# Second layer of a two-layer trunk: its first four mixing and up-projection units taken on the unnormalised input, root and shift applied to their sums, its modulation vectors all on VectorE

## The chip, the cores and the metric

The kernel runs on one core of one Trainium2 chip. The metric is device time in microseconds (us) of one execution. Engines are called as in the profile: PE is TensorE (PEld its weight loads), DVE is VectorE, ACT is ScalarE, POOL is GpSimd, SP is the engine whose queue issues nearly all DMAs.

## What is computed

Two layers run over 384 tokens (128 context, 256 latent), D = 1024. Cut to what matters here, a layer is:

```
mod = silu(cond) @ w_ada + b_ada              # six vectors: sh1, sc1, g1, sh2, sc2, g2
h   = rms(x, g_norm1) * (1 + sc1) + sh1
u   = h @ w_in                                # gates and the inputs of four token mixers
...                                           # mixers, branch projections, gated merge
x   = x + g1 * (merged @ w_out)
h2  = rms(x, g_norm2) * (1 + sc2) + sh2
x   = x + g2 * (silu(gate) * val) @ w_down    # gate, val: conv of width 3 over h2 @ w_up
```

rms divides a token by the root of its mean square. `cond` is one vector for context tokens and another for latent tokens, so each modulation vector has two columns. All is float32.

## The kernel before

**Layout.** Activations are transposed: 8 blocks (k = 0 to 7) of 128 channels by 384 tokens. Weights come as a stream of units, one unit being one block of 128 output channels: 128 x 1024 in SBUF, 512 KB. Layer l has 13 mixing units, 32 gate units, 8 branch, 8 output (`O0`), 44 up-projection (`P0`) and 24 down-projection units (`D0`, three to a block d of x). Every product is made of three: weight and activation are split in a high and a low part, and `dense` (L1439) gives PE three products per block k: high by high, high by low, low by high, so 24 products of 384 columns for a whole unit.

**Weight pipeline.** A unit passes four slots. SP loads it (`load_unit`, L478) once the unit four before is done, ACT rounds it to the high part (`split`, L687), DVE subtracts for the low part (`split`, L976), and PE waits for both in `unit_ready` (L1434). All four queues run in the order in which the program is written; nothing reorders them.

**Norms.** For layer 2's first norm and for the second norm of both layers, x gets its last block from the last `residual` (DVE, L1317). Then: ACT squares it, PE sums squares over channels with a matrix of ones (`square_sums`, L1471), ACT takes the root with Ln and Exp (L714 to L716), and then per block DVE multiplies x by scale and root (L1047), ACT adds the shift and rounds (`act_hi`, L725), DVE makes `act_lo` (L1055). PE starts the next stage with `group` (L1452), three units interleaved over k, each step waiting for its block's `act_lo`.

**Modulation.** The vectors come in two ways. Some are PE products against `cond_silu` (`modulate`, L1396, 8 blocks of 512 KB each): in layer 2 these are sh2 (`hole_units`, between the first norm's square sums and its first unit) and g2 (`norm_units`, at the same place of the second norm). The others are row products on DVE (`row_products`, L1000), two instructions for a 512 KB block, spread between the splits by `MIX_ROWS`, `STEP_ROWS` and `DOWN_LAST`; SP loads block b once the two products of block b - 2 are done (L443).

**MLP.** An up unit's bank is read by ACT (the middle tap, L914) and DVE (the outer taps, L1350 and L1354), in pairs of units; DVE finishes a column block with L1359 and L1362, then splits the next unit but one (L1363). PE may write bank j again only after the convolution of its last unit, and units `P0+4` to `P0+7` use banks 0 to 3 again (L1829).

## Time and profile before

| what | value |
|---|---|
| median of 3 runs (lowest to highest) | 1223.99 us (1223.44 to 1224.53) |
| the profiled execution | 1223.51 us |
| its span | 1221.7 us |
| PE busy | 1208.0 us, 99% of the span |
| DVE busy | 901.4 us, 74% |
| ACT busy | 575.6 us, 47% |
| POOL busy | 136.8 us, 11% |
| HBM read | 195.25 MB, 162 GB/s over the span |

The span is the part of the execution from the first to the last recorded instruction; the execution's own time is 1.8 us more. The page gives busy times of each engine; a chain of waits, followed back from the last instruction, tells what set the end; a timeline lists instructions with their start in us from the start of the span, and in brackets how long the engine sat idle before and what ended that. Layer 1 ends and layer 2 begins at about 620 us; layer 2's second norm lies at about 938 us.

### The profile page before, as it was taken

What the parts mean: (1) busy time and instruction counts of PE and PEld (TensorE: products, weight loads), DVE (VectorE), ACT (ScalarE), POOL (GpSimd) and SP (SyncE); (2) the same over time, 40 slices, a digit from 0 to 9 for tenths busy, and PEclk for the clock granted to TensorE, in tenths of its full rate; (3) what the DMA queues carried; (4) which work ended last, traced back from release to release, by engine and by line L of the source; (5) the groups of instructions that cost most, each with busy time, mean ns of one, the idle gap of its engine ahead of it and who ended that gap; (6) DMA issues with size and microseconds to landing.
All of it is one profiled execution on the core that took longest, in us unless ns stands there. A gap on an engine that the chain in (4) does not pass through costs nothing.

```text
span 1221.7 us, 19781 instructions
## 1 busy us (share of the span) xinstructions
PE 1208.0 (99%) x7816; PEld 1149.7 (94%) x7816; DVE 901.4 (74%) x1671; ACT 575.6 (47%) x949; POOL 136.8 (11%) x109
## 2 busy tenths in 40 slices
PE   8999999999999999999999999999999999999998
PEld 7987999989989999999989889999998999999998
DVE  5597877748689999986876965765686887887432
ACT  3445564643365544532354455645425554454321
POOL 0232000008300000000202500000271000000000
PEclk9999999999999999999999999999999999999999
DMA  9763433444744444469664522332345334334443
GB/s 370 291 220 125 147 117 112 172 139 161 253 173 144 167 156 159 169 216 322 214 234 163 189 87 87 104 104 87 104 167 196 122 124 135 122 123 136 134 142 121
DMA packets 53532, 198.82 MB, mean 163 GB/s; under 512 B 6784, under 2 KB 7200, under 8 KB 51904
## 3 DMA queue, kind: packets, MB, share of 16 engines
q1 hardware_dynamic: 53120, 196.86, 46.0%
q8 instruction: 63, 1.03, 0.3%
q0 software_dynamic: 320, 0.69, 0.2%
q14 instruction: 29, 0.24, 0.1%
HBM read 195.25 MB, written 2.27 MB: 162 GB/s over the span
## 4 chain that ended last, share of the span: by engine, by line
PE 93%; DVE 2%; POOL 2%; DMA 1%; issue 1%; ACT 0%; SPq 0%; DVEq 0%; POOLq 0%; ACTq 0%
PE bank L1444 27%; PE bank L1446 27%; PE bank L1445 26%; PE bank L1743 1%; PE bank L1723 1%; PE bank L1512 1%; DVE w_lo L980 1%; DMA start_ada<-start_ada 1%; PE bank L1517 1%; PE bank L1516 1%; POOL wide L653 1%; PE bank L1713 1%; POOL merge_sum L655 1%; PE bank L1501 1%; PE bank L1698 1%
## 5 line engine op out<-in xcount | busy, mean ns | idle before, releaser
L1444 PE MATMUL bank<-act_hi,w_hi 128*128 128x384 f32 x1368 | 465.0, 340 | 0.7 <-DVE act_lo L1055 0.3
L1446 PE MATMUL bank<-act_hi,w_lo 128*128 128x384 f32 x1368 | 457.8, 335 | 0.0
L1445 PE MATMUL bank<-act_lo,w_hi 128*128 128x384 f32 x1336 | 446.6, 334 | 0.0
L980 DVE TENSOR_TENSOR w_lo<-w_raw,w_hi 128x1024 fp32r<-128x1024 f32 x251 | 318.9, 1272 | 114.6 <-ACT w_hi L662 113.6
L662 ACT ACTIVATE w_hi<-w_raw 128x1024 fp32r<-128x1024 f32 x251 | 264.3, 1054 | 167.8 <-DMA w_raw<-stream 167.7
L1444 PEld LDWEIGHTS bank<-act_hi,w_hi 128*128 128x128 f32 x1368 | 257.1, 188 | 10.7 <-issue 6.5
L1446 PEld LDWEIGHTS bank<-act_hi,w_lo 128*128 128x128 f32 x1368 | 256.8, 188 | 0.0
L1445 PEld LDWEIGHTS bank<-act_lo,w_hi 128*128 128x128 f32 x1336 | 251.0, 188 | 0.6
L1446 PE MATMUL bank<-mlp_hi,w_lo 128*128 128x384 f32 x352 | 118.3, 336 | 0.0
L1444 PE MATMUL bank<-mlp_hi,w_hi 128*128 128x384 f32 x352 | 118.3, 336 | 0.0
L1445 PE MATMUL bank<-mlp_lo,w_hi 128*128 128x384 f32 x352 | 118.3, 336 | 0.0
L1350 DVE SCALAR_TENSOR_TENSOR mlp_tmp<-bank,params,mlp_tmp 128x127 f32<-128x127 f32 (+1 forms) x176 | 64.7, 409 | 38.1 <-ACT mlp_tmp L662 38.1
L662 ACT ACTIVATE mlp_tmp<-bank,params 128x384 f32<-128x384 f32 x88 | 54.2, 667 | 81.3 <-PE bank L1446 81.3
L1354 DVE SCALAR_TENSOR_TENSOR mlp_tmp<-bank,params,mlp_tmp 128x127 f32<-128x127 f32 (+1 forms) x176 | 65.2, 412 | 3.1
L1444 PEld LDWEIGHTS bank<-mlp_hi,w_hi 128*128 128x128 f32 x352 | 66.2, 188 | 0.0
L1446 PEld LDWEIGHTS bank<-mlp_hi,w_lo 128*128 128x128 f32 x352 | 66.2, 188 | 0.0
L1445 PEld LDWEIGHTS bank<-mlp_lo,w_hi 128*128 128x128 f32 x352 | 66.2, 188 | 0.0
L1011 DVE SCALAR_TENSOR_TENSOR row_products<-ada,cond_spread 128x1024 f32<-128x1024 f32 x48 | 60.9, 1270 | 0.9 <-DMA ada<-ada_rows 0.7
L1238 DVE TENSOR_REDUCE small<-bank 128x1 f32<-128x384 f32 (+1 forms) x72 | 31.3, 462 | 40.9 <-PE bank L1714 15.6
L662 ACT ACTIVATE gates_b<-bank 128x384 f32<-128x384 f32 x48 | 23.6, 492 | 67.6 <-PE bank L1446 67.3
L1011 DVE SCALAR_TENSOR_TENSOR row_products_mix<-ada,cond_spread_mix 128x1024 f32<-128x1024 f32 x38 | 50.9, 1340 | 4.0 <-DMA cond_spread_mix<-cond_rows 3.1
L653 POOL TENSOR_TENSOR wide<-wide 128x768 f32<-128x768 f32 x8 | 18.7, 2334 | 273.7 <-DVE wide L1306 273.7
(246 smaller groups left out, 1576.0 us busy)
## 6 DMA issues: line engine op xcount, KB each, us to landing
w_raw<-stream SPq DMA_DIRECT2D x251, 512.0 KB, 3.3
ada<-ada_rows SPq DMA_DIRECT2D x48, 512.0 KB, 4.4
start_ada<-start_ada SPq DMA_DIRECT2D x8, 1024.0 KB, 17.9
ada_norm<-ada_w SPq DMA_DIRECT2D x16, 512.0 KB, 5.8
ada<-ada_w SPq DMA_DIRECT2D x8, 512.0 KB, 5.5
start_raw<-start_w SPq DMA_DIRECT2D x8, 448.0 KB, 18.5
ada_head_a<-ada_w SPq DMA_DIRECT2D x5, 512.0 KB, 7.3
cond_spread_mix<-cond_rows SPq DMA_DIRECT2D x2, 1024.0 KB, 7.9
```

The costliest lines, as they stand in the source:

```text
L653: own(nc.gpsimd.tensor_tensor(g[:, 0:2, :], g[:, 0:2, :], g[:, 2:4, :], ALU.add))
L655: nc.gpsimd.tensor_tensor(msum[:, d % 4, :], g[:, 0, :], g[:, 1, :], ALU.add).then_inc(merged_ready, 1)
L662: return nc.scalar.activation(out, in_, func, **kw)
L980: V.tensor_tensor(wlo[s][:, :], raw[s][:, :], whi[s][:, :].bitcast(F32), ALU.subtract).then_inc(lo_ready, 1)
L1011: V.scalar_tensor_tensor(out[:, :], ada[b % 2][:, :], 1.0, tile[:, t, :], ALU.mult, ALU.mult, accum_out=mod[:, at, t:t + 1]).then_inc(rows ...
L1238: own(V.reduce_max(small[:, c + m:c + m + 1], bank[score_bank(i, m)][:, 0:n], AX))
L1350: own(V.scalar_tensor_tensor(f[:, m, a + 1:e], b[:, a:e - 1], before, f[:, m, a + 1:e], ALU.mult, ALU.add))
L1354: ins = V.scalar_tensor_tensor(f[:, m, a:e - 1], b[:, a + 1:e], behind, f[:, m, a:e - 1], ALU.mult, ALU.add)
L1444: T.matmul(out, wb[s][0][:, w, :], hi[k], start=first and k == 0, stop=False)
L1445: T.matmul(out, wb[s][0][:, w, :], lo[k], start=False, stop=False)
L1446: ins = T.matmul(out, wb[s][1][:, w, :], hi[k], start=False, stop=last and k == n - 1)
L1501: ins = T.matmul(bank[7][p0:p0 + STRIP, j * n:(j + 1) * n], conds[:, k, :], w[:, c:c + n], start=k == 0, stop=k == KD - 1)
```

## The change

Layer 1 computes as before. In layer 2, for both norms:

- **Four units on the unnormalised input** (`FIRST = 4`). As each block of x gets final, ACT writes x times scale to `gated_late`, rounds it to a new tile `unnormed_hi`, and DVE makes `unnormed_lo` (`unnormed_high`, `unnormed_low`). Two more columns behind the 384 hold the shift vector. PE runs the four first units one after another on these tiles, 386 columns wide, with the square sums after block 3 of the first unit (`first_units`).
- **Root and shift on the sums.** For each of the four, DVE copies the two shift columns and multiplies the 384 sums by the root (`rescale`), ACT adds the shift columns (`add_shift`), in place in the bank for the up units.
- **The normalised input** for all later units is still made: POOL multiplies `gated_late` by the root into `wide` (`normed`, 8 instructions), ACT rounds (`normed_high`), DVE makes `act_lo` (`normed_low`). These are written between the rescales and splits. The fifth unit waits for them block by block (`normed_unit`).
- **Modulation.** `hole_units` and layer 2's `norm_units` are gone from PE. sh2 and g2 of layer 2 are 16 more blocks of row products: eight more in the mixing and attention stages, eight in the up projection; the 26 row products of layer 1's down projection are the first ones again but start two units later and are spread by `DOWN_ROWS`, from a copy of the condition loaded over `act_hi`.
- Output projection block d % 4 = 3 uses bank 6 in place of bank 0.

In the diff, `act.` and `A(` stand in ACT's program, `dve.` and `V.` in DVE's, `pe.` and `dense` in PE's.

```diff
-DOWN_LAST = (2, 2, 1, 1, 1, 1, 1, 1)
+DOWN_ROWS = [0, 0] + [1 + (u in (5, 10, 15, 20)) for u in range(2, 24)]
-            {u: 1 for u in range(5, 21)})
-STEP_ROWS = ({0: 1, 1: 1, 2: 1, 3: 1, 13: 2, 14: 2, 15: 2, 16: 2, 17: 2}, {})
+            {u: 1 + (u == 10) for u in range(6, 23)})
+STEP_ROWS = ({0: 1, 1: 1, 2: 1, 3: 1, 13: 2, 14: 2, 15: 2, 16: 2, 17: 2},) * 2
-OUT_BANK = (2, 5, 4, 0)
+OUT_BANK = (2, 5, 4, 6)
...
+                def normed(n):
+                    pool.wait_ge(rstd_ready, l * 2 + n + 1)
+                    for k in range(KD):
+                        nc.gpsimd.tensor_tensor(wide[:, k, :], late[:, k, :], rsn, ALU.mult).then_inc(norm_full, 1)
...
+                def unnormed_high(n, d):
+                    for a, e, c in RANGES:
+                        ins = A(late[:, d, a:e], x[:, d, a:e], ACT.Copy, scale=(sc1, sc2)[n][:, d, c:c + 1])
+                    ins.then_inc(u_full, 1)
+                    act.wait_ge(u_full, n * KD + d + 1)
+                    A(uhi[n][:, d, 0:TOK], late[:, d, :], ACT.Copy).then_inc(u_hi, 1)
+                def add_shift(n, q, out):
+                    act.wait_ge(rescaled, n * FIRST + q + 1)
+                    for a, e, c in RANGES:
+                        ins = A(out[:, a:e], out[:, a:e], ACT.Identity, bias=sums_shift[:, q, c:c + 1])
+                    return ins
...
                         for m in range(2):
+                                add_shift(1, 2 * j + m, bank[2 * j + m]).then_inc(shifted, 1)
+                                act.wait_ge(shifted, 2 * j + m + 1)
                             A(f[:, m, :], bank[2 * j + m][:, 0:TOK], ACT.Identity,
+                        if l > 0 and i == 0 and j == 0:
+                            normed_high(1, 3)
+                            normed_high(1, 4)
                         A(f[:, 2, :], f[:, 0, :], ACT.Tanh, scale=0.5).then_inc(mlp_tanh, 1)
                         split(u + 4, i)
+                            for k in range(5, KD):
+                                normed_high(1, k)
...
+                    if l < DEPTH - 1 and u % 3 == 0 and u >= 6:
+                        d = u // 3 - 2
+                        act.wait_ge(x2_ready, FROM + l * KD + d + 1)
+                        unnormed_high(0, d)
...
+                def rescale(n, q, out):
+                    u = (0, P0)[n] + q
+                    dve.wait_ge(rstd_ready, l * 2 + n + 1)
+                    dve.wait_ge(unit_done, FROM + l * UNITS + u + 1)
+                    V.tensor_copy(sums_shift[:, q, :], bank[q][:, TOK:wide_w])
+                    V.tensor_tensor(out, bank[q][:, 0:TOK], rsn, ALU.mult).then_inc(rescaled, 1)
...
                         split(u + 3, i)
+                        if l > 0 and i == 0 and j == 0:
+                            normed_low(1, 2)
+                            rescale(1, 1, bank[1][:, 0:TOK])
+                            normed_low(1, 3)
+                            normed_low(1, 4)
+                        if l > 0 and i == 0 and j == 1:
+                            rescale(1, 2, bank[2][:, 0:TOK])
+                            rescale(1, 3, bank[3][:, 0:TOK])
...
-            def hole_units():
...
+                def first_units(n, u0, ready, counts):
+                    for q in range(FIRST):
+                        unit_ready(u0 + q)
+                        pe.wait_ge(ready, counts[q])
+                        for k in range(KD):
+                            if q == 0:
+                                pe.wait_ge(u_lo, n * (KD + 1) + k + 1 + (n == 1 or k >= 3))
+                            ins = dense(bank[q][:, 0:wide_w], u0 + q, [k], [uhi[n][:, k, :]], [ulo[n][:, k, :]], k == 0, k == KD - 1)
+                            if q == 0 and k == 3:
+                                square_sums(n)
+                        ins.then_inc(unit_done, 1)
...
-                    square_sums(0)
-                    hole_units()
-                    group(0, (0, 1, 2), HI, LO, lambda k: pe.wait_ge(norm_lo, l * 2 * KD + k + 1))
+                    first_units(0, 0, x2_ready, [FROM + KD // 2 + 1 + q for q in range(FIRST)])
```

**First place: DVE at the end of layer 1's down projection.** Before, with the last two blocks of x (`x<-bank` is a residual, `row_products` a row product, the two `w_lo` are the splits of units 0 and 1 of layer 2):

```order
L1011 SCALAR_TENSOR_TENSOR row_products,mod<-ada_65,cond_spread 128x1024 [waits rows_read,rows_loaded0]
L1319 SCALAR_TENSOR_TENSOR x<-bank,mod,x 128x128 [waits unit_done]
L1319 SCALAR_TENSOR_TENSOR x<-bank,mod,x 128x256
L1011 SCALAR_TENSOR_TENSOR row_products,mod<-ada_65,cond_spread 128x1024 [waits rows_read]
L1011 SCALAR_TENSOR_TENSOR row_products,mod<-ada_66,cond_spread 128x1024 [waits rows_read,rows_loaded1]
L1011 SCALAR_TENSOR_TENSOR row_products,mod<-ada_66,cond_spread 128x1024 [waits rows_read]
L980 TENSOR_TENSOR w_lo_59<-w_raw_60,w_hi_61 128x1024 [waits hi_ready]
L980 TENSOR_TENSOR w_lo_62<-w_raw_63,w_hi_64 128x1024 [waits hi_ready]
L1319 SCALAR_TENSOR_TENSOR x<-bank,mod,x 128x128 [waits unit_done]
L1319 SCALAR_TENSOR_TENSOR x<-bank,mod,x 128x256
```

And now:

```order
L1097 SCALAR_TENSOR_TENSOR row_products_down,mod<-ada_66,cond_spread_down 128x1024 [waits rows_read,spread_down_loaded]
L1097 SCALAR_TENSOR_TENSOR row_products_down,mod<-ada_65,cond_spread_down 128x1024 [waits rows_read,rows_loaded0]
L1432 SCALAR_TENSOR_TENSOR x<-bank,mod,x 128x128 [waits unit_done]
L1432 SCALAR_TENSOR_TENSOR x<-bank,mod,x 128x256
L1069 TENSOR_TENSOR unnormed_lo_112<-gated_late,unnormed_hi_111 128x384 [waits unnormed_hi]
L1097 SCALAR_TENSOR_TENSOR row_products_down,mod<-ada_65,cond_spread_down 128x1024 [waits rows_read,spread_down_loaded]
L1097 SCALAR_TENSOR_TENSOR row_products_down,mod<-ada_66,cond_spread_down 128x1024 [waits rows_read,rows_loaded1,spread_down_loaded]
L1097 SCALAR_TENSOR_TENSOR row_products_down,mod<-ada_66,cond_spread_down 128x1024 [waits rows_read,spread_down_loaded]
L1066 TENSOR_TENSOR w_lo_59<-w_raw_60,w_hi_61 128x1024 [waits hi_ready]
L1066 TENSOR_TENSOR w_lo_62<-w_raw_63,w_hi_64 128x1024 [waits hi_ready]
L1432 SCALAR_TENSOR_TENSOR x<-bank,mod,x 128x128 [waits unit_done]
L1432 SCALAR_TENSOR_TENSOR x<-bank,mod,x 128x256
```

Two row products instead of one stand ahead of the residual of block 6, an `unnormed_lo` piece follows it, and then come the three row products, the two splits and the last residual as before.

**Second place: SP at the same point.** Before, from the load of unit `D0+23` to that of unit 3 of layer 2 (`ada<-ada_rows` is a block for the row products):

```order
L483 DMA w_raw_54<-stream 128x1024 [waits unit_done]
L446 DMA ada_65<-ada_rows 128x1024 [waits rows_read]
L483 DMA w_raw_57<-stream 128x1024 [waits unit_done]
L483 DMA w_raw_60<-stream 128x1024 [waits unit_done]
L446 DMA ada_66<-ada_rows 128x1024 [waits rows_read]
L483 DMA w_raw_63<-stream 128x1024 [waits unit_done]
L483 DMA w_raw_54<-stream 128x1024 [waits unit_done]
L483 DMA w_raw_57<-stream 128x1024 [waits unit_done]
```

And now:

```order
L490 DMA w_raw_57<-stream 128x1024 [waits unit_done]
L490 DMA w_raw_60<-stream 128x1024 [waits unit_done]
L453 DMA ada_65<-ada_rows 128x1024 [waits rows_read]
L490 DMA w_raw_63<-stream 128x1024 [waits unit_done]
L453 DMA ada_66<-ada_rows 128x1024 [waits rows_read]
L490 DMA w_raw_54<-stream 128x1024 [waits unit_done]
L490 DMA w_raw_57<-stream 128x1024 [waits unit_done]
```

The last block of rows is issued behind the load of layer 2's unit 1, no longer ahead of it.

**Third place: DVE in layer 2's MLP**, from the split of unit `P0+3` to that of unit `P0+4`. Before:

```order
L980 TENSOR_TENSOR w_lo_59<-w_raw_60,w_hi_61 128x1024 [waits hi_ready]
L1350 SCALAR_TENSOR_TENSOR mlp_tmp<-bank,params,mlp_tmp 128x127 [waits tap1]
L1350 SCALAR_TENSOR_TENSOR mlp_tmp<-bank,params,mlp_tmp 128x255
L1354 SCALAR_TENSOR_TENSOR mlp_tmp<-bank,params,mlp_tmp 128x127 [waits dve_own]
L1354 SCALAR_TENSOR_TENSOR mlp_tmp<-bank,params,mlp_tmp 128x255
L1350 SCALAR_TENSOR_TENSOR mlp_tmp<-bank,params,mlp_tmp 128x127 [waits tap1]
L1350 SCALAR_TENSOR_TENSOR mlp_tmp<-bank,params,mlp_tmp 128x255
L1354 SCALAR_TENSOR_TENSOR mlp_tmp<-bank,params,mlp_tmp 128x127 [waits dve_own]
L1354 SCALAR_TENSOR_TENSOR mlp_tmp<-bank,params,mlp_tmp 128x255
L1359 SCALAR_TENSOR_TENSOR mlp_tmp<-mlp_tmp 128x384 [waits mlp_tanh]
L1362 SCALAR_TENSOR_TENSOR mlp_tmp<-mlp_tmp 128x384 [waits conv_val,dve_own]
L980 TENSOR_TENSOR w_lo_62<-w_raw_63,w_hi_64 128x1024 [waits hi_ready]
```

And now, up to the first outer tap (the rest, taps to `P0+4`'s split, is as before and is followed by three more pieces of `act_lo`):

```order
L1066 TENSOR_TENSOR w_lo_59<-w_raw_60,w_hi_61 128x1024 [waits hi_ready]
L1133 SCALAR_TENSOR_TENSOR act_lo<-wide,mod,act_hi 128x128 [waits norm_hi]
L1133 SCALAR_TENSOR_TENSOR act_lo<-wide,mod,act_hi 128x256
L1153 COPY cond_raw<-bank 128x2 [waits unit_done,rstd_ready]
L1154 TENSOR_TENSOR bank<-bank,rstd 128x384
L1133 SCALAR_TENSOR_TENSOR act_lo<-wide,mod,act_hi 128x128 [waits norm_hi]
L1133 SCALAR_TENSOR_TENSOR act_lo<-wide,mod,act_hi 128x256
L1133 SCALAR_TENSOR_TENSOR act_lo<-wide,mod,act_hi 128x128 [waits norm_hi]
L1133 SCALAR_TENSOR_TENSOR act_lo<-wide,mod,act_hi 128x256
L1483 SCALAR_TENSOR_TENSOR mlp_tmp<-bank,params,mlp_tmp 128x127 [waits tap1]
```

Between the split and the taps stand three pairs of `act_lo` and a rescale. The second column block has two rescales between the split of `P0+5` and its taps.

## Rows read from the trace of the kernel before

**Rows 1.** The page: busy time of each engine.

```profile
PE 1208.0 (99%) x7816; PEld 1149.7 (94%) x7816; DVE 901.4 (74%) x1671; ACT 575.6 (47%) x949; POOL 136.8 (11%) x109
```

**Rows 2.** The chain of waits, 615 to 640 us: start, length, what.

```profile
620.16 0.75 DVE x L1319 x2
...
621.37 1.05 ACT w_hi L662
622.44 1.23 DVE w_lo L980
623.73 0.76 DVE wide L1047 x2
624.57 0.81 ACT act_hi L662 x2
625.48 0.76 DVE act_lo L1055 x2
626.27 0.44 PE bank L1444
```

**Rows 3.** Timeline of PE where layer 2 begins: start, busy, engine, line, operation.

```profile
619.96 0.81 PE L1474 MATMUL bank<-wide,consts 128*128 128x384 f32 x2
620.61 0.81 PE L1476 MATMUL bank<-wide,consts 128*128 128x384 f32 x2
```

**Rows 4.** Timeline of DVE, then PE, where layer 2's MLP begins.

```profile
933.57 0.74 DVE L1319 SCALAR_TENSOR_TENSOR x<-bank,mod,x 128x128 f32<-128x128 f32 x2 [2.29 <-PE bank L1446]
...
937.73 0.74 DVE L1319 SCALAR_TENSOR_TENSOR x<-bank,mod,x 128x128 f32<-128x128 f32 x2 [2.28 <-PE bank L1446]
...
937.53 0.81 PE L1474 MATMUL bank<-wide,consts 128*128 128x384 f32 x2
...
943.69 0.44 PE L1444 MATMUL bank<-act_hi,w_hi 128*128 128x384 f32 x1
```

**Rows 5.** Timeline of DVE at the end of layer 1's down projection.

```profile
609.99 1.93 DVE L980 TENSOR_TENSOR w_lo<-w_raw,w_hi 128x1024 fp32r<-128x1024 f32 x1 [1.11 <-ACT w_hi L662]
611.84 1.21 DVE L1011 SCALAR_TENSOR_TENSOR row_products<-ada,cond_spread 128x1024 f32<-128x1024 f32 x1
...
612.98 0.73 DVE L1319 SCALAR_TENSOR_TENSOR x<-bank,mod,x 128x128 f32<-128x128 f32 x2
...
617.38 2.35 DVE L980 TENSOR_TENSOR w_lo<-w_raw,w_hi 128x1024 fp32r<-128x1024 f32 x2
```

**Rows 6.** Timeline of SP at the same place; the page's row on the ada rows.

```profile
609.09 0.43 SPq L446 DMA_DIRECT2D ada<-ada_rows  x1
612.88 7.61 SPq L483 DMA_DIRECT2D w_raw<-stream  x3
...
ada<-ada_rows SPq DMA_DIRECT2D x48, 512.0 KB, 4.4
```

**Rows 7.** Timeline of ACT: a table load; the middle taps of two up units.

```profile
609.97 1.28 ACT L666 ACT_TABLE_LOAD   x1
...
960.67 1.21 ACT L662 ACTIVATE mlp_tmp<-bank,params 128x384 f32<-128x384 f32 x2
```

**Rows 8.** Timeline of DVE in the first two column blocks of layer 2's MLP.

```profile
959.17 1.22 DVE L980 TENSOR_TENSOR w_lo<-w_raw,w_hi 128x1024 fp32r<-128x1024 f32 x1
960.31 0.55 DVE L983 TENSOR_TENSOR mlp_lo<-mlp_tmp,mlp_hi 128x384 fp32r<-128x384 f32 x1
...
961.94 0.73 DVE L1350 SCALAR_TENSOR_TENSOR mlp_tmp<-bank,params,mlp_tmp 128x127 f32<-128x127 f32 x2
...
965.85 1.22 DVE L980 TENSOR_TENSOR w_lo<-w_raw,w_hi 128x1024 fp32r<-128x1024 f32 x1
```

**Rows 9.** Timeline of POOL, then DVE: instructions alone and beside each other.

```profile
609.82 1.01 POOL L589 TENSOR_TENSOR wide<-wide 128x384 f32<-128x384 f32 x1
...
907.06 2.18 DVE L1289 SCALAR_TENSOR_TENSOR merged_lo<-merge_sum,merged_hi 128x384 fp32r<-128x384 f32 x1
910.70 0.56 DVE L1289 SCALAR_TENSOR_TENSOR merged_lo<-merge_sum,merged_hi 128x384 fp32r<-128x384 f32 x1 [1.47 <-ACT merged_hi L662]
```

More of the change, by code:

```diff
@@ L361, in program @@
         norm_ada_loaded = [sem(f"norm_ada_loaded{n}") for n in range(2)]
-        hole_ada_loaded = [sem(f"hole_ada_loaded{n}") for n in range(2)]
+        spread_down_loaded, scale_ready = sem("spread_down_loaded"), sem("scale_ready")
+        u_full, u_hi, u_lo, rescaled = sem("unnormed_full"), sem("unnormed_hi"), sem("unnormed_lo"), sem("rescaled")
+        shifted = sem("shifted")
         rows_loaded = [sem(f"rows_loaded{n}") for n in range(2)]
@@ L719, in norm @@
+                def norm(n):
+                    roots(n)
                     for k in range(KD):
-                        if n == 0 and l == 0:
+                        if n == 0:
                             start_high(k)
                             act.wait_ge(start_shift, k + 1)
-                        act.wait_ge(norm_full, (l * 2 + n) * KD + k + 1)
-                        for a, e, c in RANGES:
-                            ins = A(ahi[:, k, a:e], wide[:, k, a:e], ACT.Identity, bias=shift[:, k, c:c + 1])
@@ L756, in _ @@
                     if name in SQUARED:
-                        i, rows = SQUARED.index(name), NOPE if name == "cqr" else P
-                        act.wait_ge(mix_out, l * U_MIX + u + 1)
-                        A(wide[0:rows, i, :], pj[0:rows, PJ[name], :], ACT.Square).then_inc(psq, 1)
+                        mix_squares(u)
                 def gate(g):
@@ L1102, in _ @@
                 else:
-                    dve.wait_ge(shift_ready, l)
-                    norm(0)
-                    modulation(l, 3)
+                    for u in range(FIRST):
+                        rescale(0, u, pj[:, PJ[MIX[u]], :])
+                        normed_low(0, 2 * u)
+                        if u < FIRST - 1:
+                            split(u + 3)
+                        normed_low(0, 2 * u + 1)
                 def lambdas():
@@ L1363, in _ @@
                         split(u + 4, i)
+                        if l > 0 and i == 0 and j == 0:
+                            for k in range(5, KD):
+                                normed_low(1, k)
                         dve.wait_ge(mlp_hi, p + 1)
@@ L1519, in start_products, with normed_unit @@
                             ins.then_inc(unit_done, 1)
+                def first_units(n, u0, ready, counts):
[9 more added lines that the diff above has]
+                        ins.then_inc(unit_done, 1)
+                def normed_unit(out, u, n):
+                    unit_ready(u)
+                    for k in range(KD):
+                        pe.wait_ge(norm_lo, (l * 2 + n) * KD + k + 1)
+                        ins = dense(out, u, [k], HI[k:k + 1], LO[k:k + 1], k == 0, k == KD - 1)
+                    ins.then_inc(unit_done, 1)
                 if l == 0:
```

286 lines of the change are left out of this document (185 added, 101 removed).

## The prediction

> **What bounds the kernel now.** I read the page first: PE is busy 99% of the span, DVE 74%, ACT 47% [rows 1]. So only what PE executes, and the few stretches in which it waits, can move the end. The second view is the chain of waits where layer 2 begins. It leaves PE and runs, one after another, through the last residual, ACT's high part of a weight unit, DVE's low part, and then the norm's own steps: `wide`, `act_hi`, `act_lo`, first product [rows 2]. The third view, PE's timeline, gives the length: the square sums start at 619.96 and follow each other every 0.65 us, so three take 1.95; the first dense product starts at 626.27 [rows 2, 3]. That is a hole of 6.31 us, in which the removed `hole_units` only fill time. At the second norm of layer 2 it is 937.53 to 943.69, 6.16 us [rows 4]. DVE's residuals there lie 4.16 us apart, which is a full unit of 24 products, 0.173 us each [rows 4]. Everything below is measured against this beat.
>
> **What a perfect change would bring.** The sums stay on PE (1.95 us). Without any wait the holes shrink to that: 6.31 - 1.95 = 4.4 us and 6.16 - 1.95 = 4.2 us. The modulation products of layer 2 stood inside the holes, so their removal is in these numbers and is no gain of its own. The question is what is late next. Both places must be walked through queue by queue.
>
> **First place, start of layer 2.** PE wants unit 0 at 619.96. Before, DVE split units 0 and 1 together from 617.38 to about 619.7, the first done near 618.55 [rows 5]. Now its queue is longer: one more row product ahead of the residual of block 6, 1.25 us (before, three of them fill the time from the residual's end, 613.64, to 617.38 [rows 5]); one `unnormed_lo` piece, 0.5 us (nearest row: a low part of the same size, 0.55 busy [rows 8]). Besides, the last block of rows is issued behind the unit load of 612.88 and no longer at 609.09; at 4.4 us to landing it is there at 617.7 [rows 6], while DVE wants it at 612.98 + 1.25 + 0.7 + 0.5 + 1.25 = 616.7. That is 1.0 us more. Sum: 618.55 + 1.25 + 0.5 + 1.0 = 621.3. ACT isn't later: after the residual (615.0) it has the scaled block and its rounding, 0.81 + 0.55, the table load, 1.28, and the high part, 1.05, thus 618.7 [rows 2, 7]. So PE waits 1.35 us (bounds: 0.3 if the block lands in time, 2.3 if it needs a microsecond more), and the hole shrinks by 6.31 - 1.95 - 1.35 = 3.0 us. The last block of x costs nothing: PE needs it only as step 7 of unit 0, some 6 us after its start, and ACT and DVE need 3 to 4 us from the last residual.
>
> The four units then end at 621.3 + 1.95 + 4 x 4.16 = 639.9. Unit 4 needs the third rescaled sum out of the way. From the root (628) DVE has three rescales (0.7 each, taken as a low part of 384 elements and a small copy; bounds 0.5 and 1.1, two such), four `act_lo` pairs of 0.76 and two splits of 1.2: 7.5 us, 635.5 [rows 2, 8]. But POOL now runs its eight products in the same time. **What POOL costs DVE** the trace shows: beside a POOL add, a split took 1.93 in place of 1.22, and a 384-element low part 2.18 in place of 0.56 [rows 5, 8, 9]. I take 0.7 us for each of the six pieces: 639.7, and with ACT's shift, 0.81 [rows 2], 640.5. PE waits 0.6 us (bounds 0 and 2). The two added columns cost 192 x 2/384 x 0.173 = 0.2 us over both places, 0.1 here. First place: -3.0 + 0.6 + 0.1 = **-2.3 us** (-4.4 to -0.5).
>
> **Second place, start of layer 2's MLP.** PE starts unit `P0` at 937.53 with no wait: the DMA queue lost eight modulation blocks there, and DVE's splits have 2.3 us of idle time around each residual [rows 4]. The four units end at 937.53 + 1.95 + 16.64 = 956.1, before at 943.69 + 16.64 = 960.3. Then `P0+4` needs its low part. Before, that split ran 959.17 to 960.31 [rows 8]: ready in the very moment. It stands in DVE's queue behind the convolution of units 0 and 1, and now four more things stand ahead of that. Step by step: sums done 941.6, root 942.7, table load to 944.0 [rows 7], three `act_hi` and the high part of `P0+3` to 947.5; DVE's split to 948.7, `act_lo` and rescale of unit 1 to 950.2; then back to ACT: shift 0.81, tap 0.6, two `act_hi` 1.6, to 953.2 [rows 2, 7]; back to DVE: `act_lo` to 954.0, taps and the rest of the column block 3.9 us (961.94 to 965.85 [rows 8]), to 957.9, split to 959.1. With POOL beside it for two of these pieces and more, 1.4 us, **960.5**. So the part that gates PE is as late as before: of the 4.2 us nothing is left (bounds: 959.1 without POOL, 962 with it throughout).
>
> And the queue is longer in the next half block too. Before, from the split of `P0+4` to the end of that of `P0+6` were 960.31 to 967.0, 6.7 us [rows 8], against two units, 8.3 us. Now: three `act_lo` 2.2, low part 0.5, split 1.15, one rescale, the shift and the tap behind it 2.1 (the other rescale beside them), taps and rest 3.9, split 1.15: 11.0 us. PE waits 2.7 us, `P0+6` starts at 960.5 + 11.0 = 971.5, before at 960.3 + 8.3 = 968.65. Second place: **+2.8 us** (+1.3 to +4.3). Afterwards a half block takes DVE 6.7 us, with a row product 7.9, against 8.3: it catches up, and the eight blocks of row products that come into this stage cost nothing. Those in mixing and attention go to places where layer 1's tables already have as many; if that cover is gone, each costs its 1.25 us.
>
> **The sum.** 1223.5 (the profiled execution) - 2.3 + 2.8 = 1224.0. That execution lies 0.5 below the median of the runs, so **1224.5 us**. A measurement of this kernel can tell about 0.2%, 2.4 us, from no change; this is inside it. By its own bounds this case reaches from 1221.5 to 1228.
>
> **Rivals.** (1) *The queues keep up*, faster. If the pieces of ACT and DVE overlap better than I chain them and the low part of `P0+4` is ready at 956 to 957, `P0+6` is in time too; the second place gives up to -4.2 and the first -3: 1216.8. For it: DVE has 26% idle in all [rows 1]. Against: DVE and ACT wait for each other in turn through shift, tap, `act_hi`, `act_lo`, and the split was just in time even before [rows 8].
> (2) *POOL locks DVE out*, slower. The eight POOL products stand back to back, about 1.0 us each [rows 9], from 942.7 on. If every DVE instruction with two SBUF inputs waits for the end of one of them, as the 2.18 us row suggests [rows 9], the split of `P0+3` and the three pairs ahead of the second rescale are later by some 3 us and not 1.4, and unit 4 of layer 2 waits 2 us longer: second place +4.5, first -0.3, 1228.2. It decides once `P0+4`'s low part comes after 962. The Trainium skill, "SBUF — State Buffer", section "SBUF: two separate sides", says that VectorE with two SBUF inputs and GpSimd take a shared port pair for the whole instruction and the other one fully blocks; by that rule the time is this rival's. The forecast takes the smaller price because of the eight pieces only some meet an add at its start, and sums in PSUM take one SBUF input.
> (3) *The 386-column form is slow.* If it ran at the square sums' beat, 0.325 a product in place of 0.173 [rows 3, 4], 192 of them would cost 29 us: 1253. Same operands and type speak against it.
>
> **How the numbers follow.** The forecast's case has 0.52: 0.38 within 0.2%, 0.10 slower, 0.04 faster, since its bounds lean upward. Rival 1 has 0.24, rival 2 0.21, rival 3 0.03. So faster 0.28, same 0.38, slower 0.34. The range, 1218.5 to 1229.0, takes in the forecast's bounds and rival 2, and leaves out the far half of rival 1 and rival 3.
>
> **What would show it.** In the new profile PE should start layer 2's unit 0 about 1.3 us after the last down product, waiting for `w_lo`, and unit `P0` with no wait. It should wait for DVE `w_lo` about 4.4 us ahead of `P0+4` (956.1 to 960.5, shifted by the 2.3 us won) and 2.7 us ahead of `P0+6`; those two waits are the forecast. Products of 386 columns should come every 0.174 us. DVE splits beside POOL's eight products should take about 1.9 us. I am wrong if either MLP wait is missing, if PE waits inside a first unit for `unnormed_lo`, or if a wait appears in attention, where rows were added.

## The result, and the profile after

The changed kernel takes **1233.32 us** (median of 4 runs, 1231.78 to 1234.43), the kernel before, on the same chip, 1223.81 (1223.44 to 1224.53): a ratio of 1.0075, 95% interval 1.0062 to 1.0087. It is 9.5 us slower. The prediction said 1224.5, which is almost no change, and a range up to 1229.0. The forecast is wrong and the range misses the time by 4.3 us.

The page of the changed kernel answers [rows 1]: PE lost a point, DVE is 46 us busier, and the granted clock of PE, full in every slice before, is not full in one of the 40 slices.

```profile
PE 1206.8 (98%) x7688; PEld 1150.2 (93%) x7688; DVE 947.1 (77%) x1735; ACT 597.4 (48%) x1011; POOL 154.0 (12%) x125
...
PEclk9999999999999999999999999999999899999999
```

The view by windows says where. Columns: window, length, busy time and instructions of PE, PEld, DVE, ACT and POOL, then PE's granted clock, DMA share and GB/s.

```profile
620.00:630.00 10.00, 8.09 (x33) 6.66 (x32) 6.30 (x10) 5.52 (x10) 0.58 (x1) 0.83 0.86 326
630.00:640.00 10.00, 10.00 (x58) 10.00 (x57) 9.32 (x12) 7.12 (x17) 9.45 (x12) 1.00 0.54 184
640.00:650.00 10.00, 7.36 (x39) 6.28 (x37) 9.95 (x16) 5.11 (x13) 7.43 (x7) 1.00 0.29 100
...
960.00:970.00 10.00, 4.31 (x15) 4.02 (x14) 9.89 (x24) 5.17 (x11) 0.00 (x0) 0.74 0.16 53
```

Three stretches lose, and DVE is full in two of them. PE's timeline shows both kinds of loss, waits and pace. The products of one unit follow each other every 0.18 us until 623.41, and from there every 0.32, although nothing is waited for:

```profile
622.28 0.41 PE L1581 MATMUL bank<-unnormed_hi,w_hi 128*128 128x386 f32 x1 [1.91 <-ACT w_hi L673]
...
623.06 0.34 PE L1582 MATMUL bank<-unnormed_lo,w_hi 128*128 128x386 f32 x1
...
623.41 0.52 PE L1581 MATMUL bank<-unnormed_hi,w_hi 128*128 128x386 f32 x1
623.73 0.52 PE L1582 MATMUL bank<-unnormed_lo,w_hi 128*128 128x386 f32 x1
...
648.16 0.44 PE L1581 MATMUL bank<-act_hi,w_hi 128*128 128x384 f32 x1 [2.24 <-DVE act_lo L1133]
649.35 0.44 PE L1581 MATMUL bank<-act_hi,w_hi 128*128 128x384 f32 x1 [0.40 <-DVE act_lo L1133]
...
966.35 0.66 PE L1581 MATMUL bank<-act_hi,w_hi 128*128 128x384 f32 x1 [5.69 <-DVE w_lo L1066]
...
1037.30 0.41 PE L1581 MATMUL bank<-act_hi,w_hi 128*128 128x384 f32 x1 [1.72 <-ACT w_hi L673]
```

The slow pace is the lower of TensorE's two levels, 1.2 GHz in place of 2.4; this text calls it half pace. Behind the first wait it lasts about 3.4 us, from 623.4 to 626.8, and costs 1.7: from the start of unit 0 to its 14th product, square sums included, PE takes 5.9 us (622.28 to 628.18), and 4.24 for the same work at the second place (941.54 to 945.78). Behind 966.35 it lasts 5.2 us and costs 2.5.

The profile puts the wait of 1.91 us down to ACT's `w_hi`. Unit 0 had its high part at 620.38; its low part, the first of the two splits here, stands behind the last row product and was ready near 622.1:

```profile
619.80 1.23 DVE L1097 SCALAR_TENSOR_TENSOR row_products_down<-ada,cond_spread_down 128x1024 f32<-128x1024 f32 x1
620.95 2.36 DVE L1066 TENSOR_TENSOR w_lo<-w_raw,w_hi 128x1024 fp32r<-128x1024 f32 x2
```

Unit 4 starts without a wait, at 643.02, and stops 15 products later, at block 5 of the normalised input. Its `act_lo` is the last line here, and the three pieces run beside POOL's window sums of mixing:

```profile
642.05 2.17 DVE L1133 SCALAR_TENSOR_TENSOR act_lo<-wide,mod,act_hi 128x128 fp32r<-128x128 f32 x2
644.14 1.88 DVE L1066 TENSOR_TENSOR w_lo<-w_raw,w_hi 128x1024 fp32r<-128x1024 f32 x1
645.94 2.16 DVE L1133 SCALAR_TENSOR_TENSOR act_lo<-wide,mod,act_hi 128x128 fp32r<-128x128 f32 x2
```

How late each mark is against the kernel before gives the account (starts of instructions, in us; the last column adds up what came in since the mark above):

| mark | before | after | late | what came in between |
|---|---|---|---|---|
| last down product of layer 1 starts | 619.79 | 620.03 | 0.2 | before the places; not explained |
| mixing, product behind the root | 674.90 | 678.41 | 3.5 | wait 1.9, half pace 1.7, unit 4's waits 2.6, wait for the root 0.45, wide columns 0.4, some 0.6 in short pauses around the waits; less the 4.4 of the hole |
| `P0`, before the square sums ahead of it, starts | 937.53 | 941.54 | 4.0 | short waits that before doesn't have, the longest 0.3 at 924.8 |
| unit `P0+4` starts | 960.49 | 966.35 | 5.9 | wait 5.7, columns 0.4; less the 4.2 |
| unit `P0+6` starts | 968.89 | 977.16 | 8.3 | half pace 2.5 |
| end of the span | 1221.7 | 1232.6 | 10.9 | wait 1.7 at 1037 |

(Of the last line 0.9 us is not accounted for.) DVE's timeline at the second place shows what takes its time while POOL runs its eight products, 947.0 to 956.4:

```profile
949.09 2.22 DVE L1133 SCALAR_TENSOR_TENSOR act_lo<-wide,mod,act_hi 128x128 fp32r<-128x128 f32 x2 [2.59 <-ACT act_hi L673]
951.24 0.14 DVE L1153 COPY cond_raw<-bank 128x2 f32<-128x2 f32 x1
951.30 0.55 DVE L1154 TENSOR_TENSOR bank<-bank,rstd 128x384 f32<-128x384 f32 x1
951.77 1.75 DVE L1133 SCALAR_TENSOR_TENSOR act_lo<-wide,mod,act_hi 128x128 fp32r<-128x128 f32 x2
953.44 2.05 DVE L1066 TENSOR_TENSOR w_lo<-w_raw,w_hi 128x1024 fp32r<-128x1024 f32 x1
955.40 1.50 DVE L1133 SCALAR_TENSOR_TENSOR act_lo<-wide,mod,act_hi 128x128 fp32r<-128x128 f32 x2
...
947.02 9.34 POOL L597 TENSOR_TENSOR wide<-gated_late,rstd 128x384 f32<-128x384 f32 x8 [6.64 <-ACT rstd L673]
```

A pair of `act_lo` is 0.75 [rows 2], a split 1.22 [rows 8]. The four pieces are late by 1.5 + 1.0 + 0.8 + 0.75 = 4.0 us. The rescale, which reads one of its inputs from PSUM, keeps its 0.55. The Trainium skill, "SBUF — State Buffer", section "SBUF: two separate sides", says that of a VectorE instruction with two SBUF inputs and a GpSimd instruction that reads SBUF the one that starts first holds their shared ports to its end, and the other is blocked. The trace agrees: a POOL product takes 1.17 us here, and a pair of `act_lo`, two instructions, takes up to 2.22 us in place of 0.75.

### The profile page after: what moved, and what is told of

It reads as the page before. It is cut to its first block, busy times and chain, and to the rows that moved or that the text cites. A ratio compares the mean times of both kernels' runs of the same rounds, so it can differ in the third digit from the quotient of the medians.

```text
span 1232.6 us, 19718 instructions
## 1 busy us (share of the span) xinstructions
PE 1206.8 (98%) x7688; PEld 1150.2 (93%) x7688; DVE 947.1 (77%) x1735; ACT 597.4 (48%) x1011; POOL 154.0 (12%) x125
## 3 DMA queue, kind: packets, MB, share of 16 engines
q8 instruction: 62, 1.02, 0.3%
HBM read 197.35 MB, written 2.27 MB: 162 GB/s over the span
## 4 chain that ended last, share of the span: by engine, by line
PE 87%; DVE 6%; DMA 4%; ACT 2%; issue 1%; SPq 0%; POOL 0%; DVEq 0%; ACTq 0%
PE bank L1581 25%; PE bank L1583 24%; PE bank L1582 24%; DMA w_raw<-stream 2%; DVE w_lo L1066 2%; DVE act_lo L1133 1%; PE bank L1902 1%; PE bank L1882 1%; PE bank L1649 1%; DMA start_ada<-start_ada 1%; PE bank L1654 1%; PE bank L1653 1%; PE bank L1872 1%; ACT w_hi L673 1%; PE bank L1638 1%
## 5 line engine op out<-in xcount | busy, mean ns | idle before, releaser
L1581 PE MATMUL bank<-act_hi,w_hi 128*128 128x384 f32 x1304 | 445.3, 341 | 10.3 <-DVE w_lo L1066 5.7
L1583 PE MATMUL bank<-act_hi,w_lo 128*128 128x384 f32 x1304 | 437.4, 335 | 0.0
L1582 PE MATMUL bank<-act_lo,w_hi 128*128 128x384 f32 x1272 | 426.3, 335 | 0.0
L1581 PEld LDWEIGHTS bank<-act_hi,w_hi 128*128 128x128 f32 x1304 | 245.9, 189 | 21.2 <-issue 14.0
L1583 PEld LDWEIGHTS bank<-act_hi,w_lo 128*128 128x128 f32 x1304 | 245.5, 188 | 0.0
L1582 PEld LDWEIGHTS bank<-act_lo,w_hi 128*128 128x128 f32 x1272 | 239.8, 189 | 0.6
L1097 DVE SCALAR_TENSOR_TENSOR row_products_mix<-ada,cond_spread_mix 128x1024 f32<-128x1024 f32 x44 | 55.1, 1253 | 4.4 <-DMA cond_spread_mix<-cond_rows 3.7
L673 ACT ACTIVATE mlp_tmp<-mlp_tmp 128x384 f32<-128x384 f32 x44 | 23.1, 525 | 61.0 <-DVE mlp_tmp L1487 61.0
```

The lines of the kernel that those rows point to most:

```text
L673: return nc.scalar.activation(out, in_, func, **kw)
L1097: V.scalar_tensor_tensor(out[:, :], ada[b % 2][:, :], 1.0, tile[:, t, :], ALU.mult, ALU.mult, accum_out=mod[:, at, t:t + 1]).then_inc(rows ...
L1581: T.matmul(out, wb[s][0][:, w, :], hi[k], start=first and k == 0, stop=False)
L1582: T.matmul(out, wb[s][0][:, w, :], lo[k], start=False, stop=False)
L1583: ins = T.matmul(out, wb[s][1][:, w, :], hi[k], start=False, stop=last and k == n - 1)
```

## The experiments

All diffs are against the changed kernel and abridged. Each ratio is against the kernel before, run on the same chip; its medians there are 1223.8 to 1224.3 us. Differences between two variants are taken from their medians; where the two intervals overlap, as for several below, the time alone does not separate them. The traces show single executions.

**e1: only the modulation moved.** Both norms as before, the row products where the change has them.

```diff
-                    first_units(0, 0, x2_ready, ...)
+                    square_sums(0)
+                    group(0, (0, 1, 2), HI, LO, lambda k: pe.wait_ge(norm_lo, l * 2 * KD + k + 1))
```

> Both norms of layer 2 as in the kernel before (no unit on the unnormalised input), but the modulation stays on VectorE as in the change, so that each hole holds nothing but three square sums: PE is idle for about 4.3 us in it. Theory 'clock' (PE loses its granted clock behind an idle stretch and runs at half pace for some 4 to 5 us, which costs 2.2 to 2.6 us): 1223.8 + 2 x 2.4 = 1228.6, and with the late weight unit behind the rows of the MLP, 1.7, 1230.3; slices behind both holes show a granted clock under 1. Rival 'the modulation is free and the clock is set by something else': 1223.8 to 1225.5, granted clock 1.00 throughout.

Measured 1232.02 (ratio 1.0063, 1.0048 to 1.0078), above even the first theory. **Taking the modulation off PE, with the new places of its row products, costs 8 us by itself.** Windows of PE alone:

```profile
620.00:630.00 10.00, 3.53 (x11) 0.80 0.94 351
630.00:640.00 10.00, 10.00 (x52) 0.86 0.12 48
...
950.00:960.00 10.00, 10.00 (x50) 0.83 0.11 46
```

The rest comes from DVE and PE around the first hole:

```profile
622.44 0.73 DVE L1471 SCALAR_TENSOR_TENSOR x<-bank,mod,x 128x128 f32<-128x128 f32 x2
...
623.78 0.91 PE L1672 MATMUL bank<-wide,consts 128*128 128x384 f32 x2 [2.69 <-ACT wide L683]
628.48 0.69 PE L1638 MATMUL bank<-act_hi,w_hi 128*128 128x384 f32 x1 [3.78 <-DVE act_lo L1156]
```

The last residual comes at 622.44, before at 620.16 [rows 2]: one more row product and two waits for its block (0.64 and 0.70) stand ahead of it. Behind the holes PE runs at the low level, which costs 2.1 us at the first and 1.7 at the second, and in mixing it waits 1.1 us for a root.

**e5: the same, with the holes filled.** The products of constants return to PE what the modulation did for it: something to run.

```diff
+                    for _ in range(16):
+                        T.matmul(bank[7][:, 0:P], cc("ones"), cc("ones"), start=True, stop=True)
```

> The kernel of e1 (both norms as before, modulation on VectorE) with 16 small products of constants behind the square sums of each norm of layer 2 (3.5 us of the 3.8 that PE waits there). Theory 'clock': nothing is earlier or later on VectorE and ScalarE, only the half pace behind the holes goes: granted clock 1.00, 1232.0 - 4.2 = 1227.8; what is left against before (3.5 to 4) are the last residual of layer 1, 2.3 us late behind a row product, and the 1.1 us for the root in mixing. Rival 'the time of e1 is the row products alone': 1231 to 1232.

Measured 1228.63 (1.0041, 1.0026 to 1.0056): 3.4 us less than e1, from products that compute nothing (the intervals of the two overlap a little). The second hole is followed by full clock; the first still has a slice at 0.83, since the fill stands behind a wait of 2.8 us inside the sums.

```profile
620.00:630.00 10.00, 7.21 (x37) 0.83 0.85 318
630.00:640.00 10.00, 10.00 (x62) 1.00 0.22 90
...
950.00:960.00 10.00, 10.00 (x60) 1.00 0.09 22
```

**e2: fill in the changed kernel** (8 products ahead of unit 0, 25 behind the bank's wait of `P0+4`).

> The change, with 8 small products of constants ahead of layer 2's unit 0 (1.7 us) and 25 ahead of unit P0+4 (5.4 us), into a bank nobody reads: they lie inside the waits that the changed kernel has there (1.9 and 5.7 us). Theory 'clock': the waits stay, the half pace behind them goes, granted clock 1.00, 1233.3 - 4.8 = 1228.5. Rival 'the clock falls for another reason' (the 386-column products, the DMA load): same clock record, 1233 to 1234.

Measured 1231.25 (1.0057, 1.0042 to 1.0072); in the profiled execution the clock is 1.00 throughout. 2.1 us came back and not 4.8, and the interval overlaps that of the changed kernel. The filler of the second place started only at 961.28, when the bank was free, and ran 2 us past the low part; e8 mends that.

**e8: the fill where PE really stands** (24 products ahead of that wait).

> e2 with the filler of the second place (24 products, 5.2 us) ahead of the wait for bank 0, where PE really stands, so that it ends before the low part comes. Theory 'clock': 2.2 us (first place) and 2.6 us (second place) come back in full, 1228.5; in e2 the filler ran 961.3 to 966.9, 2.1 us beyond the low part. Rival 'the second place has no clock loss of its own': 1231.

Measured 1233.51 (1.0074, 1.0059 to 1.0089): nothing. Its trace is the most telling of all:

```profile
966.44 0.41 PE L1638 MATMUL bank<-act_hi,w_hi 128*128 128x384 f32 x1 [0.30 <-DVE w_lo L1089]
977.15 0.41 PE L1638 MATMUL bank<-act_hi,w_hi 128*128 128x384 f32 x1 [2.12 <-DVE w_lo L1089]
```

Full clock behind 966.44, and `P0+6` then waits 2.1 us for its low part and starts at 977.15, where the changed kernel has 977.16. The half pace there had only hidden the wait of the forecast. At the first place the low level now came behind unit 4's wait instead (slices of 0.96 and 0.87 from 640).

**e9: GpSimd's presence alone.**

```diff
-                        nc.gpsimd.tensor_tensor(wide[:, k, :], late[:, k, :], rsn, ALU.mult).then_inc(norm_full, 1)
+                        nc.gpsimd.tensor_tensor(wide[:, k, 0:2], late[:, k, 0:2], rsn[:, 0:2], ALU.mult).then_inc(norm_full, 1)
```

> The change, with GpSimd multiplying only 2 of the 384 columns of each block of a norm of layer 2 by the root (the other columns reach the high and low parts with whatever wide holds): its eight operations take next to nothing, and nobody else does their work. It leaves out the normalisation of those columns. It prices GpSimd's presence alone. Theory 'port': VectorE's pairs and splits beside GpSimd return to 0.75 and 1.22 us, some 4 us at each norm; unit 4's wait goes, P0+4's falls from 5.7 to about 2; P0+6 waits 0 to 1: 1233.3 - 2.6 - 2.2 - 3.7 = 1225 to 1227. Rival 'chain of shift, tap and split': P0+4 waits 4 us or more all the same, 1230.

The other 382 columns are not normalised here: e9 is a price and not a version.

Measured 1225.47 (1.0017, 1.0007 to 1.0026), 10 runs: **of the 9.5 us, 7.9 are gone once eight operations a norm shrink, on an engine that is idle 88% of the time.** Not all of that is POOL's. The two traces lie 8.8 us apart. Of these, 0.5 stands already at the last down product; 1.7 is the half pace of the first place, which did not follow here although PE waited 2.12 us ahead of unit 0, all before POOL's first product at 627.56; and 1.7 is the wait at 1037, which e1 and e3 lack too. About 4.9 us are left, 3.7 of them between the start of `P0` and that of `P0+6`. That is what POOL's products do to VectorE and, since ScalarE's `act_hi` waits for each, their own length. The clock is 1.00 throughout in this trace. The same pieces as above, and what is left of the waits:

```profile
946.33 0.75 DVE L1179 SCALAR_TENSOR_TENSOR act_lo<-wide,mod,act_hi 128x128 fp32r<-128x128 f32 x2 [2.59 <-ACT act_hi L686]
...
948.66 1.23 DVE L1112 TENSOR_TENSOR w_lo<-w_raw,w_hi 128x1024 fp32r<-128x1024 f32 x1 [0.40 <-ACT w_hi L686]
```

```profile
960.00 0.41 PE L1696 MATMUL bank<-act_hi,w_hi 128*128 128x384 f32 x1 [2.09 <-DVE w_lo L1112]
970.71 0.41 PE L1696 MATMUL bank<-act_hi,w_hi 128*128 128x384 f32 x1 [2.14 <-DVE w_lo L1112]
```

2.1 + 2.1 us: just what the hole had given. Even with GpSimd's products away the second place gains nothing.

**e3: the eight products on VectorE.**

> The change, with the eight products x times root of each norm of layer 2 on VectorE in place of GpSimd. Theory 'port' (VectorE with two SBUF inputs waits for GpSimd's operation): pairs of act_lo 0.75 us in place of 1.2 to 2.4, unit 4's wait of 2.6 us goes, the wait ahead of P0+4 falls from 5.7 to 2 to 4 us; 1233.3 - 2.6 - 2.5 = 1228. Rival 'length of the queue': VectorE has 16 more operations of 0.5 us, 4 us a norm, which eat what the pairs give back: both waits as long as now or longer, 1233 to 1236.

Measured 1229.7 (1.0041, 1.0026 to 1.0056). The pairs are 0.75 us again, except beside POOL's window sums of mixing, the products take 3.9 us a norm, and the whole is 3.6 us faster than the changed kernel: 3.9 us of own work is cheaper than GpSimd beside it. `P0+4` waits 3.98, with half pace behind it (0.66 from 960 to 970).

```profile
964.49 0.66 PE L1638 MATMUL bank<-act_hi,w_hi 128*128 128x384 f32 x1 [3.98 <-DVE w_lo L1089]
```

**e7 and e11: order at the second place.** In e7 only the split of `P0+4` moves ahead of the convolution (on ScalarE also that of `P0+6`).

> The change, with unit P0+4's split on both engines ahead of the convolution of units 0 and 1 in place of behind it (and P0+6's ahead on ScalarE). Theory 'the split stands behind the column block': PE then waits for bank 0 in place of the low part, until 963.5 in place of 966.3, 2.8 us less, half pace stays: 1230.5. Rival 'it only trades places, since the bank is as late as the split': 1233.

Measured 1233.72 (1.0079, 1.0064 to 1.0094). `P0+4` waits 3.91 in place of 5.69, now for its bank, as foretold, and `P0+6` waits 2.81: the wait moved.

```profile
964.92 0.44 PE L1638 MATMUL bank<-act_hi,w_hi 128*128 128x384 f32 x1 [3.91 <-DVE mlp_tmp L1535]
978.30 0.41 PE L1638 MATMUL bank<-act_hi,w_hi 128*128 128x384 f32 x1 [2.81 <-DVE w_lo L1089]
```

e11 is e3 with a whole new order:

```diff
+                    for k in range(3): normed(1, k)
+                    rescale(1, 0, bank[0][:, 0:TOK]); split(P0 + 3); normed_low(1, 0)
+                    normed(1, 3); normed(1, 4); normed_low(1, 1); normed_low(1, 2)
+                    rescale(1, 1, bank[1][:, 0:TOK])
+                    for k in range(5, KD): normed(1, k)
+                    conv(0, 0, 0); split(P0 + 4); normed_low(1, 3); normed_low(1, 4)
+                    conv(0, 0, 1); split(P0 + 5)
+                    for k in range(5, KD): normed_low(1, k)
```

> e3 (eight products of each norm on VectorE) with the pieces at layer 2's up projection in another order on VectorE and ScalarE: rescale of unit 1 and the convolution of units 0 and 1 and the splits of P0+4 and P0+5 between the low parts, in the order in which PE wants them. The same operations, other places. Theory 'order': the wait ahead of P0+4 falls from 4.0 to under 1.5 and with it the half pace, P0+6 waits 1 to 2: 1229.7 - 2.5 - 1.5 = 1225.7. Rival 'VectorE's work alone is the bound there' (some 17 us of it in the 18.6 us that PE needs for four units): waits trade places, 1228 to 1230.

Measured 1227.49 (1.0037, 1.0023 to 1.0050). The profiled execution is the slowest of the five, 1231.27. In it `P0+4` and `P0+5` no longer wait, `P0+6` waits 3.25 and has the low clock behind it.

```profile
971.50 0.66 PE L1695 MATMUL bank<-act_hi,w_hi 128*128 128x384 f32 x1 [3.25 <-DVE w_lo L1111]
```

The median is 2.2 below e3's, which the intervals do not separate. Both theories are half right: the wait ahead of `P0+4` is gone, another stands behind it, and it is still VectorE's.

**e6 and e10: the rows at the end of layer 1.** e6 puts the last three row products behind the last residual, and unit 0's split ahead of the scaled block on ScalarE.

> The change, with the last row products of layer 1 (the gate's last blocks, which nobody needs for 200 us) behind the last residual in place of ahead of it, and unit 0's split ahead of the scaled block on ScalarE. Theory 'first place is set by the row products in VectorE's queue': PE's wait of 1.9 to 2.1 us ahead of unit 0 falls to 0 to 0.5 us, no half pace behind it: 1233.3 - 1.7 - 2.2 = 1229.4. Rival 'the DMA queue sets it' (the weight unit itself is late): the wait stays, 1233.

Measured 1234.82 (1.0091, 1.0074 to 1.0108), slower. Unit 0 doesn't wait, but PE then waits 1.70 inside it for `unnormed_lo`, 1.71 ahead of unit 3, whose low part is ready only near 638.4, and 3.68 for the rescaled sums. The edit is not quite clean: the row products' scratch lies over `act_hi`, so ScalarE had to wait for them (7.4 us idle), and they now ran beside GpSimd, 1.9 us each in place of 1.22. Still, moving a piece inside the full stretch only moved the wait.

```profile
627.58 0.44 PE L1638 MATMUL bank<-unnormed_hi,w_hi 128*128 128x386 f32 x1 [1.70 <-DVE unnormed_lo L1092]
638.61 0.42 PE L1638 MATMUL bank<-unnormed_hi,w_hi 128*128 128x386 f32 x1 [1.71 <-issue]
646.77 0.44 PE L1638 MATMUL bank<-act_hi,w_hi 128*128 128x384 f32 x1 [3.68 <-ACT proj L683]
```

e10 takes four blocks out of the stretch, into mixing and attention:

```diff
-MLP_BLOCKS = len(ROWS)
+MLP_BLOCKS = len(ROWS) - 4
-DOWN_ROWS = [0, 0] + [1 + (u in (5, 10, 15, 20)) for u in range(2, 24)]
+DOWN_ROWS = [int(2 <= u < 20) for u in range(24)]
```

> The change, with four blocks of row products (half of the gate of layer 2's attention) moved from the last units of layer 1 into mixing and attention of layer 2, so that VectorE has no row product behind unit 19 of the down projection. Unlike e6 they leave the whole stretch from 600 to 650 us. Theory 'rows ahead of the last residuals': unit 0's split is there when PE wants it, wait under 0.5, and the half pace behind it goes: 1233.3 - 1.7 - 2.2 = 1229.4. Rival 'the wait comes back': PE waits for the later pieces as in e6 (unnormed_lo, unit 3, unit 4), or in mixing behind the added rows: 1232 to 1234.

Measured 1230.86 (1.0060, 1.0043 to 1.0076). No wait at unit 0, none inside the first four units, no low clock there; 1.1, 1.1 and 0.6 us at unit 4. The 2.5 us less are the best figure for what the late rows cost, with intervals that overlap.

**e4: rows in the MLP** issued half a group later by SyncE.

```diff
+                        if l and i >= 2 and j == 1:
+                            load_rows_behind(2, len(ROWS))
```

> The change, with the two row blocks of each group of four MLP units of layer 2 issued half a group later (behind the second unit load of the next group), so that SyncE does not stand waiting for VectorE's row product with unit loads behind it. Theory 'queue of SyncE': the wait of 1.7 us for w_hi at 1037 goes, SyncE's waits for row products fall from 50 us to under 20, 1231.6. Rival 'that unit was late from contention on the DMA engines': the wait stays, 1233.3.

Measured 1232.66 (1.0066, 1.0049 to 1.0083), 0.7 less than the changed kernel, which the intervals don't separate. In the trace the wait at 1037 is gone and so are SyncE's waits for `row_products` of this stage, of which the changed kernel has (total, times, longest, in us)

```profile
SPq L453 <- DVE row_products L1097: 50.4, 6, 10.6
```

Unit loads were queued behind them. That they made the wait at 1037 is not shown: the traces of e1 and e3 have as much of these waits, 47.5 and 48.4 us, and no such wait on PE. (Waits of 1 to 2 us for `w_hi` turned up at other places in e5, e8 and e11.)

**e13, e14: one place at a time.** The other norm as before, with an empty hole.

> The change at the first norm of layer 2 alone; the second norm as in the kernel before (its hole holds three square sums and nothing else), modulation on VectorE. From e1's trace the old second norm costs 0.1 for the hole and 2.1 for the half pace behind it, from the changed kernel's trace the new one 4.6: 1233.3 - 2.4 = 1231. Rival 'the first place is the smaller part': 1228.

> The change at the second norm of layer 2 alone, the first as before with an empty hole, modulation on VectorE. From e1's trace the old first norm costs 2.2 (late residual) + 2.1 (half pace) + 1.1 (root in mixing) = 5.4, the new one 3.5, so 1233.3 + 1.9 = 1235. Rival 'the second place is where the change loses': 1234 or less, with e13 at 1228.

Measured 1230.73 (1.0056, 1.0041 to 1.0071) and 1233.78 (1.0081, 1.0064 to 1.0097). Against e1, 1232.02: the first place alone is worth -1.3, the second alone +1.8, both +1.3. The intervals of e1, e13 and e14 overlap, so these signs are not shown. What is clear is that neither place earns back the 8 us of the moved modulation. e13's wait of 2.25 us ahead of unit 0 had no half pace behind it in its trace.

**e12 and e15: all together.** e12 is e10 and e11 in one.

> e10 and e11 together: rows out of the end of layer 1, eight products on VectorE, pieces in the new order. If the two places are independent: 1229.4 + 1225.7 - 1229.7, with e3's first place in it, 1222 to 1225. If the backlog of VectorE is carried: 1227.

Measured 1230.64 (1.0056, 1.0041 to 1.0071), no better than either alone. In its trace, of the fastest execution (1228.20), unit 4 waits 2.4 + 0.8 + 0.4, `P0+6` 3.25. e15 adds e9's two columns.

> The bound of the idea: e9 (GpSimd multiplies 2 of 384 columns, the normalisation of the others left out), with e10's rows moved and e11's order. Nothing disturbs VectorE, and it does none of the eight products. Theory 'what is left is VectorE's own extra work and the rows': unit 0 without wait, unit 4 under 1, P0+4 and P0+6 together under 2; 1225.5 - 2 - 2.5 = 1221, faster than before by 0.2%. Rival 'queues other than VectorE set it': 1224 to 1225, and then no order of these pieces makes the idea pay.

Measured 1226.20 (1.0020, 1.0010 to 1.0029), slower than either theory and no faster than e9 alone (1225.47). Unit 0 has no wait, unit 4 has 1.04, 1.09 and 0.64. In part the rival holds: ACT waits 5.1 us for a unit's load that SyncE issued at 627.5 and that landed 8.3 us later. The parameters (926 KB), the caches, two row blocks and the condition's copy (1 MB) had been issued at 621.7 to 624.2, and the DMA engines are full from 625 to 635 (shares 1.02 and 0.96). In the second place `P0+6` still waits 2.94, and that is VectorE.

```profile
635.80 1.06 ACT L687 ACTIVATE w_hi<-w_raw 128x1024 fp32r<-128x1024 f32 x1 [5.11 <-DMA w_raw<-stream]
```

No version here beats the kernel before, this one with GpSimd's share left out included.

## Why the prediction was wrong

**"A hole of 6.31 us, in which the removed `hole_units` only fill time."** This step failed first. The fill kept PE's clock. Once it is gone, waits can be followed by the low level (e1, e5), which the sum has at nothing. At the first place it cost 1.7 us. At the second it cost 2.5 on paper, but e8 shows that there it hides the wait ahead of `P0+6`.

It is not the whole miss, and not its largest part. The span grew by 10.9 us in the profiled execution, where the sum had 0.5. Of these 10.4 us, 5.6 arose at the first place (half pace 1.7, unit 4's waits 2.0 more than forecast, unit 0's 0.6, the rest in small terms), 0.5 up to `P0`, 1.5 at the second place, and 2.8 lie outside both: 0.2 ahead of the first, and behind the second the wait at 1037 and 0.9 not accounted for.

**First place, forecast -2.3, measured +3.3** (3.5 late, 0.2 of it already there). Wait for unit 0: 1.35 forecast, 1.91 measured, its mechanism (row product, block landing late) right: row products at 614.66 and 618.46 waited 0.97 and 0.31 for their blocks. Half pace: 0 against 1.7. Unit 4: 0.6 against 2.6, and here the path was wrong. The forecast stopped at the third rescaled sum, which was out of the way in time; the wait came at block 5 of the normalised input, which it did not follow. The 0.7 us a piece beside POOL came out in the sum (4.7 us for the six pieces against 4.2) and not piece by piece: the first two pairs took 1.7 and 1.5 more, the first split 0.8. Two things were left out: ACT's `act_hi` also waits for POOL's products, and when they end, POOL's windows for mixing take over, at 639 to 648, with pairs of 2.17 and 2.16 again. Wide columns: 0.1 against 0.4, as a product of 386 follows the last after 0.178 us and not 0.174. Mixing: "cost nothing" against a wait of 0.45 for the root, and 1.1 in e1 and e9; that the added rows cause it was not tested.

**Second place, forecast +2.8, measured +4.3 up to `P0+6`.** The walk through the two queues held: forecast waits 4.4 and 2.7, measured 5.7, and 2.1 once the clock is full (e8). From `P0+4` to `P0+6` it had 11.0 us, e8 has 10.7. What was mis-sized is "POOL beside it for two of these pieces and more, 1.4 us": it is 4.0, and the second rescale is done 15.9 us after the start of `P0` where the walk without POOL had 12.7. Counted from the same start, the low part is ready after 24.6 us; the forecast had 23.0, and rival 2 decided from 24.5 on. **Rival 2 was the right case here**, with its +4.5 (its -0.3 at the first place was not), and its chance of 0.21 too small. Its rule was named and then set aside for a smaller price; the four pieces above show the full one, and e9 shows them back at 0.75 and 1.23 without it. That the whole, 1233.3, lies beyond this rival's 1228.2 comes from the other terms.

**"The eight blocks of row products that come into this stage cost nothing."** The DVE time was hidden, as said. SyncE's queue was not looked at; it stands 50.4 us behind these rows, but that this made the wait of 1.7 us at 1037 stays open (e4).

**Rival 1**, 1216.8, is not reached even with GpSimd and the late rows out of the way (e15, fastest of ten 1224.51). Rival 3 is wrong: 386 columns cost 0.004 us more.

One error runs through these terms, and it is one of bookkeeping; this part is argued from the sums. The forecast priced each extra piece on VectorE against the slack around it, place by place. Per norm the kernel before has 8 pairs of scaling and 8 of `act_lo`, 16 x 0.66 = 10.6 us. The change has 8 `unnormed_lo` at 0.5, 4 rescales at 0.6 and 8 `act_lo` pairs, 11.7, and POOL beside them costs 4 more. So the queue that had made the holes got longer, not shorter, though most `unnormed_lo` run ahead of the root, in time that VectorE had. In e6, e7, e11 and e12 a wait taken out of it came back behind.

## What to carry to other kernels

Before taking filler work off the engine that sets the end, ask what that engine does in the hole instead: a bare wait can cost its length and a stretch at half clock behind it. Work given to an idle engine is not free if it shares a port with the one that is late: price it for every piece beside it, not for a few meetings. And where one in-order queue feeds the critical engine, sum that queue over the whole stretch before and after; if the sum grows, expect a new order to move the waits and not to remove them, as it did here.
